# One channel tile of the depthwise convolution moves from VectorE to ScalarE and GpSimd, and the rotated queries get a new layout

## What is computed

```
h = rmsnorm(x, attn_norm_g)
q, k, v, conv_in, gate_logits = split(h @ w_in)        # 16 query heads of 64, 2 key/value heads
q, k = rope(q), rope(k)
y_attn = sliding_window_sink_attention(q, k, v) @ w_attn_o   # chunks of 64, window of 2 chunks
ca, cb = split(conv_in)
u = ca * sigmoid(cb)
u = causal_dwconv(u, conv_dw_w, conv_dw_b)             # 31 taps, one weight per channel and tap
y_conv = silu(layernorm(u)) @ w_conv_o
merged = sigmoid(g_attn) * y_attn + sigmoid(g_conv) * y_conv
x = x + merged @ w_out
h = rmsnorm(x, ffn_norm_g)
up = causal_dwconv(h @ w_ffn_up, ffn_dw_w)             # 3 taps
x = x + (silu(gate half) * value half) @ w_ffn_down
```

## Time and profile before

| what | value |
|---|---|
| median of three runs | 874.62 us (872.26 to 875.6) |
| the profiled execution, its own time | 872.64 us |
| its span, first to last instruction | 870.9 us |
| granted TensorE clock, mean | 0.994 of full speed |
| busy PE, DVE, ACT, POOL | 844.4, 627.4, 489.5, 396.4 us |
| instructions | 16394 |
| DMA | 142.26 MB, 163 GB/s |

### The profile page before, as it was taken

The page is one execution under the profiler, slowest core; times in us unless marked ns, Lnnn a source line. Parts: engine busy times, 40 slices in busy tenths (PEclk is TensorE's granted clock), DMA queues, the critical chain, the costliest instruction groups (busy, mean ns, idle before and its releaser), DMA issues.

```text
span 870.9 us, 16394 instructions
## 1 busy us (share of the span) xinstructions
PE 844.4 (97%) x6780; PEld 825.4 (95%) x6780; DVE 627.4 (72%) x1204; ACT 489.5 (56%) x754; POOL 396.4 (46%) x99
## 2 busy tenths in 40 slices
PE   8899999899999999999989999999999999999996
PEld 8899999799999999999979999989999999999996
DVE  6999999564568875666567899992636887666564
ACT  6536777473465464555563476774545555555452
POOL 4786656477403224222458785556571224222320
PEclk9999999999999999999999999999999999999999
DMA  7655433344454655554435544433454455554521
GB/s 262 207 192 170 170 129 119 140 145 146 146 195 145 198 189 194 193 172 170 148 126 211 180 160 146 146 131 113 145 190 135 160 194 194 194 183 161 191 96 49
DMA packets 22394, 142.26 MB, mean 163 GB/s; under 512 B 2736, under 2 KB 3248, under 8 KB 5808
## 3 DMA queue, kind: packets, MB, share of 16 engines
q1 hardware_dynamic: 21888, 140.96, 47.2%
q10 hardware_dynamic: 432, 0.26, 0.1%
HBM read 140.15 MB, written 1.05 MB: 162 GB/s over the span
## 4 chain that ended last, share of the span: by engine, by line
PE 66%; DVE 25%; ACT 6%; issue 2%; DMA 1%; POOL 1%; SPq 0%; DVEq 0%; ACTq 0%
PE pu L826 17%; PE pu L827 16%; PE pu L828 16%; DVE pc L594 11%; ACT whi L252 3%; DVE wlo L725 2%; PE ps L826 2%; PE ps L828 2%; PE ps L827 2%; PE ps L847 2%; PE po L847 2%; DVE qk L768 2%; PE pc L828 1%; PE pc L827 1%; PE pc L826 1%
## 5 line engine op out<-in xcount | busy, mean ns | idle before, releaser
L223 POOL TENSOR_TENSOR wlo<-raw,whi 128x2048 fp32r<-128x2048 f32 x83 | 382.6, 4612 | 435.9 <-ACT whi L252 435.9
L252 ACT ACTIVATE whi<-raw 128x2048 fp32r<-128x2048 f32 x129 | 245.5, 1903 | 19.0 <-PE pu L828 17.8
L826 PE MATMUL pu<-uh,whi 128*128 128x256 f32 x864 | 247.0, 286 | 3.5 <-DVE wlo L725 2.0
L827 PE MATMUL pu<-ul,whi 128*128 128x256 f32 x864 | 244.4, 283 | 0.0
L828 PE MATMUL pu<-uh,wlo 128*128 128x256 f32 x864 | 244.4, 283 | 0.0
L826 PE MATMUL pu<-hh,whi 128*128 128x256 f32 x768 | 221.6, 289 | 9.5 <-POOL wlo L223 5.9
L827 PE MATMUL pu<-hl,whi 128*128 128x256 f32 x768 | 218.7, 285 | 0.0
L828 PE MATMUL pu<-hh,wlo 128*128 128x256 f32 x768 | 218.5, 285 | 0.0
L594 DVE SCALAR_TENSOR_TENSOR pc<-upad,par_all,pc 128x256 f32<-128x256 f32 x464 | 186.5, 482 | 0.3
L826 PEld LDWEIGHTS pu<-uh,whi 128*128 128x128 f32 x864 | 165.7, 192 | 5.3 <-issue 4.9
L827 PEld LDWEIGHTS pu<-ul,whi 128*128 128x128 f32 x864 | 165.8, 192 | 0.2
(11 more groups left out here) (159 smaller groups left out, 1179.7 us busy)
## 6 DMA issues: line engine op xcount, KB each, us to landing
raw<-in_weights SPq DMA_DIRECT2D x129, 1024.0 KB, 4.9
raw<-in_weights SPq DMA_DIRECT2D x12, 256.0 KB, 7.0
x<-in_x_t SPq DMA_DIRECT2D x4, 256.0 KB, 5.2
out_y<-qk SPq DMA_DIRECT2D x4, 256.0 KB, 2.4
par_all<-in_params SPq DMA_DIRECT2D x1, 236.0 KB, 7.0
par_all<-in_params ACTq DMA_DIRECT2D x1, 236.0 KB, 2.4
probs<-in_positions SPq DMA_DIRECT2D x1, 128.0 KB, 6.8
const<-in_const SPq DMA_DIRECT2D x1, 64.0 KB, 7.2
```

Of the source, the lines that this page charges most:

```text
L223: nc.gpsimd.tensor_tensor(wlo[s][:, :], raw[s][:, :], whi[s][:, :].bitcast(f32), ALU.subtract).then_inc(lo_ready[s], 1)
L252: A(whi[s][:, :], raw[s][:, :], ACT.Copy).then_inc(hi_ready[s], 1)
L826: MM(out, whi[s][:, w], hi, start=start, stop=False, skip_group_check=accumulate)
L827: MM(out, whi[s][:, w], lo, start=False, stop=False, skip_group_check=accumulate)
```

## The change

Tile 2 of the eight leaves VectorE. ScalarE makes its 31 tap products, two to an instruction pair (`tap_product`), called from `next_high` at fourteen units of each layer, behind the copy of the weights; the first call makes two pairs and the last makes a pair and the single last tap. GpSimd adds each pair of 128 x 512 to a pair of sums (`add_products`), behind its subtraction for the same unit, then folds the two sums and adds the last product (`end_products`). ScalarE waits for the third addition back before it reuses one of three product buffers. VectorE has the pairs (0, 1), (3, 4), (5, 6) and then tile 7 alone as two half sums, 16 steps, the last of them an addition of the halves: 109 steps. In the softmax stage it does three steps where it did four. `mean_pair(1)` on TensorE waits for GpSimd's result as well.

The products and sums live in `qk[:, 2048:4096]`. To free that, `qr` becomes 128 partitions of 2048 columns: each rotated head stays on its own rows, so the addition of the rotation is one instruction of 128 rows for a query unit, and the keys are written twice, to both halves of the rows, by four instructions where there were two. Each scores matmul of 64 x 128 becomes two of 64 x 64, for the rows and the output partitions of the even and of the odd head.

```diff
-CONV_STEPS = TAPS * NT // 2
+CONV_PAIRS, POOL_TILE, LAST_TILE = ((0, 1), (3, 4), (5, 6)), 2, 7
+FIRST_TAPS = (TAPS + 1) // 2
+CONV_STEPS = TAPS * len(CONV_PAIRS) + FIRST_TAPS
+CONV_DONE = (2 * TAPS, 4 * TAPS, 6 * TAPS, 2 * CONV_STEPS)
+PRODUCT_BUFFERS = 3
+PRODUCT_UNITS = (7, 8, 9, 10, 11, 12, 14, 16, 17, 18, 19, 20, 21, 22)
+PRODUCTS = (TAPS + 1) // 2
+ADDITIONS = PRODUCTS - 1
...
-        qr = qk[0:HEAD_DIM, :].rearrange("p (i c o t) -> p i c o t", i=N_PAIRS, c=N_CHUNKS, o=2)
+        qr = qk[:, 0:2048].rearrange("p (i t) -> p i t", i=N_PAIRS)
+        two_sums = qk[:, 2048:2560].rearrange("p (a t) -> p a t", a=2)
+        products = [qk[:, 2560 + 512 * b:3072 + 512 * b].rearrange("p (a t) -> p a t", a=2) for b in range(PRODUCT_BUFFERS)]
-        kr = sb("kr", [HEAD_DIM, N_KV, T])
+        kr = sb("kr", [P, N_KV, T])
...
+            def add_products(l, n):
+                pool.wait_ge(tap_products, l * PRODUCTS + n + 2)
+                if n:
+                    pool.wait_ge(products_added, l * ADDITIONS + n)
+                nc.gpsimd.tensor_tensor(two_sums, two_sums, products[n % PRODUCT_BUFFERS], ALU.add).then_inc(products_added, 1)
+            def end_products(l):
+                n = PRODUCTS - 2
+                pool.wait_ge(products_added, l * ADDITIONS + n)
+                nc.gpsimd.tensor_tensor(two_sums[:, 0, :], two_sums[:, 0, :], two_sums[:, 1, :], ALU.add).then_inc(products_added, 1)
+                pool.wait_ge(tap_products, l * PRODUCTS + n + 2)
+                pool.wait_ge(products_added, l * ADDITIONS + n + 1)
+                nc.gpsimd.tensor_tensor(cv[:, POOL_TILE, :], two_sums[:, 0, :], products[n % PRODUCT_BUFFERS][:, 0, :], ALU.add).then_inc(pool_conv, 1)
...
                         split_low(s, l * USES + r)
+                        if r * RING + s in PRODUCT_UNITS:
+                            add_products(l, PRODUCT_UNITS.index(r * RING + s))
+                        if r * RING + s == PRODUCT_UNITS[-1]:
+                            end_products(l)
...
+                if u + RING in PRODUCT_UNITS:
+                    n = PRODUCT_UNITS.index(u + RING)
+                    if n == 0:
+                        tap_product(l, 0)
+                    tap_product(l, n + 1)
+                    if n == PRODUCTS - 3:
+                        tap_product(l, n + 2)
+            def tap_product(l, n):
...
+                if n == 0:
+                    act.wait_ge(par_ready, l * 5 + 1)
+                    act.wait_ge(u_ready, l * NT + POOL_TILE + 1)
+                elif n > PRODUCT_BUFFERS:
+                    act.wait_ge(products_added, l * ADDITIONS + n - PRODUCT_BUFFERS)
+                out = two_sums if n == 0 else products[(n - 1) % PRODUCT_BUFFERS]
+                for k in range(2 * n, min(2 * n + 2, TAPS)):
...
+                        last = A(out[:, k % 2, :], src, ACT.Copy, scale=w)
+                last.then_inc(tap_products, 1)
...
+                            if k == TAPS:
+                                dve.wait_ge(conv_step, l * 2 * CONV_STEPS + 2 * n + j)
+                                V.tensor_tensor(cv[:, t, :], pc[:, 0, :], cv[:, t, :], ALU.add).then_inc(conv_step, 1)
+                                continue
...
-                    for odd in range(2):
-                        rows = slice(64 * odd, 64 * odd + 64)
-                        split = [v[rows].rearrange("p n (c t) -> p n c t", c=N_CHUNKS) for v in (a, b)]
-                        V.tensor_tensor(outs[odd], split[0], split[1], ALU.add).then_inc(rope_done, 1)
+                    for rows, out in outs:
+                        last = V.tensor_tensor(out, a[rows], b[rows], ALU.add)
+                    last.then_inc(rope_done, 2)
...
-                    taps = (4, 4)
+                    taps = (3, 3)
...
-                        last = MM(bank[:, j, 0:keys.stop - keys.start], qr[:, GROUP_PAIRS * g + j, c, :, :],
-                                  kr[:, g, keys], start=True, stop=True)
+                        for odd in range(2):
+                            rows = slice(64 * odd, 64 * odd + 64)
+                            last = MM(bank[rows, j, 0:keys.stop - keys.start],
+                                      qr[rows, GROUP_PAIRS * g + j, CHUNK * c:CHUNK * c + CHUNK], kr[rows, g, keys], start=True, stop=True)
...
-                    sum_pair(ps[0][:, 0, :], cv, p, conv_step, (l * (NT // 2) + p + 1) * 2 * TAPS)
+                    if p == POOL_TILE // 2:
+                        pe.wait_ge(pool_conv, l + 1)
+                    sum_pair(ps[0][:, 0, :], cv, p, conv_step, l * 2 * CONV_STEPS + CONV_DONE[p])
```

More of the change, by code:

```diff
@@ L44 @@
 TAPS = CONV_WIDTH
-CONV_STEPS = TAPS * NT // 2
+CONV_PAIRS, POOL_TILE, LAST_TILE = ((0, 1), (3, 4), (5, 6)), 2, 7
[6 more added lines that the diff above has]
+ADDITIONS = PRODUCTS - 1
+assert len(PRODUCT_UNITS) == PRODUCTS - 2
 ROUNDING = 1.5 * 2.0 ** 23
@@ L141, in hybrid_encoder @@
         glu_tanh, u_ready, conv_step = sem("glu_tanh"), sem("u_ready"), sem("conv_step")
+        tap_products, products_added, pool_conv = sem("tap_products"), sem("products_added"), sem("pool_conv")
         kv_raw, rot_done, rope_ab, rope_done = sem("kv_raw"), sem("rot_done"), sem("rope_ab"), sem("rope_done")
@@ L256, in next_high @@
                     split_high(l, (u + RING) % RING, (u + RING) // RING)
+                if u + RING in PRODUCT_UNITS:
[6 more added lines that the diff above has]
+            def tap_product(l, n):
+                at = l * NPAR + PA_CW + POOL_TILE * CONV_WIDTH
+                bias = par_all[:, l * NPAR + PA_CB + POOL_TILE:l * NPAR + PA_CB + POOL_TILE + 1]
+                if n == 0:
[5 more added lines that the diff above has]
+                for k in range(2 * n, min(2 * n + 2, TAPS)):
+                    src, w = upad[:, POOL_TILE, k:k + T], par_all[:, at + k:at + k + 1]
+                    if k == 0:
+                        last = A(out[:, 0, :], src, ACT.Identity, scale=w, bias=bias)
+                    else:
+                        last = A(out[:, k % 2, :], src, ACT.Copy, scale=w)
+                last.then_inc(tap_products, 1)
             def high_piece(s, p):
@@ L581, in conv @@
                     for n in range(first, last):
-                        pair, k = n // TAPS, n % TAPS
+                        pair = n // TAPS
                         for j in range(2):
-                            t = 2 * pair + j
+                            if pair < len(CONV_PAIRS):
+                                t, k, begins, ends = CONV_PAIRS[pair][j], n % TAPS, n % TAPS == 0, n % TAPS == TAPS - 1
+                            else:
+                                t, k = LAST_TILE, n % TAPS + FIRST_TAPS * j
+                                begins, ends = n % TAPS == 0, k == TAPS - 1
+                            if k == TAPS:
+                                dve.wait_ge(conv_step, l * 2 * CONV_STEPS + 2 * n + j)
+                                V.tensor_tensor(cv[:, t, :], pc[:, 0, :], cv[:, t, :], ALU.add).then_inc(conv_step, 1)
+                                continue
                             w = par[:, PA_CW + t * CONV_WIDTH + k:PA_CW + t * CONV_WIDTH + k + 1]
@@ L588, in conv @@
                                 dve.wait_ge(conv_step, l * 2 * CONV_STEPS + 2 * n + j - 1)
-                            if k == 0:
+                            if begins:
                                 dve.wait_ge(u_ready, l * NT + t + 1)
+                            if begins and k == 0:
                                 V.tensor_scalar(sums, upad[:, t, 0:T], w, par[:, PA_CB + t:PA_CB + t + 1], ALU.mult, ALU.add).then_inc(conv_step, 1)
+                            elif begins:
+                                V.tensor_scalar(sums, upad[:, t, k:k + T], w, None, ALU.mult).then_inc(conv_step, 1)
                             else:
-                                out = sums if k < TAPS - 1 else cv[:, t, :]
+                                out = cv[:, t, :] if ends else sums
                                 V.scalar_tensor_tensor(out, upad[:, t, k:k + T], w, sums, ALU.mult, ALU.add).then_inc(conv_step, 1)
@@ L619, in rotate @@
                     dve.wait_ge(rope_ab, l * 10 + 2 * n + 2)
-                    for odd in range(2):
-                        rows = slice(64 * odd, 64 * odd + 64)
-                        split = [v[rows].rearrange("p n (c t) -> p n c t", c=N_CHUNKS) for v in (a, b)]
-                        V.tensor_tensor(outs[odd], split[0], split[1], ALU.add).then_inc(rope_done, 1)
+                    for rows, out in outs:
+                        last = V.tensor_tensor(out, a[rows], b[rows], ALU.add)
+                    last.then_inc(rope_done, 2)
                 dve.wait_ge(act_table, 2)
                 dve.wait_ge(kv_raw, l + 1)
-                rotate(0, pu[U_KV % RING][:, 0:1, :], 1, HEAD_DIM ** -0.5, [kr[:, g:g + 1, :].rearrange("p n (c t) -> p n c t", c=N_CHUNKS) for g in range(N_KV)])
```

(3 more changed lines are left out.)

## The result

The changed kernel takes 866.54 us (median of 4 runs, 865.75 to 868.95) against 874.05 for the kernel before in the same measurement: ratio 0.9917, 95% interval 0.9899 to 0.9935. With more rounds, in another measurement, it was 867.89 against 874.41: 0.993, 0.9913 to 0.9947. All runs of the two kernels together: 867.48 (10 runs) and 874.43 (52 runs), a difference of 6.9 us.

A forecast was written before the change was run, and what follows sets the result against it. TensorE was taken as the bound, busy 844.4 of 870.9 us. From the profiled 872.64 us, -2.0 for stalls and 0 for scores gave 870.6, moved to 872.6 against the median 874.62; range 868.5 to 880.

The forecast's parts named there:

- most of the 13 us less a layer on VectorE: Convolution and rotation: some 13 us a layer leave VectorE, nearly all beside a full TensorE, worth nothing by itself.
- ScalarE's and GpSimd's work is hidden: Products and additions of tile 2: taken as 0; the mean's second pair covered by 2 to 3 us.
- the tiles work side by side: Scores: two column tiles run together, so eight records in each take what eight took, 0 us.
- the stalls of group 7: TensorE's waits before group 7's transposes and the values behind: 1.2 us back in layer 0, 0.8 in layer 1, together 2.0.
- The 4.9 us that I gave to layer 0: Layer 0, transposes of group 6 to group 7: 5.33 us becomes 4.50 plus 0.4 for ScalarE's later copy.
- I take 0 for the 16 groups.: Scores of all groups: twice the matmuls in two tiles side by side cost and save nothing, 0 us.
- the lower end, -2 us: Scores from below: with 64 keys the time halves, 4 x -0.5 = -2 us.
- a rival with 0.10: Faster side: all softmax stalls go and short scores get shorter, 4.4 + 2 = 6.4 us, 868.2; chance 0.10.
- 4.4 us is the most that a free VectorE can give back: TensorE's softmax waits: 3.1 us for the output's low part and 1.3 for the probabilities, each twice, cap the gain.
- the sum: Whole kernel: profiled 872.64 us with -2.0 + 0 gives 870.6; 2.0 under the median, so 872.6 against 874.62.
- TensorE's waits for VectorE's softmax results are two.: Softmax stage: one wait at the end of each layer's stage; between 100 and 150 us TensorE doesn't stop.
- The two rules of the Trainium skill: Scores: loads overlap only other row groups (878 us, chance 0.08); different row tiles cannot share a PSUM bank, making turns.

The follow-up runs named there:

- The layout alone: Kernel before with only the new layout of rotated queries and keys and scores in 64 x 64 tiles, whole convolution on VectorE: 871.03 us, ratio 0.9959.
- the products alone: Changed kernel with the old layout, four scores matmuls of 64 x 128 a group, products in a tile of their own: 869.65 us, ratio 0.9952.

## Why the prediction was wrong

Right: TensorE is the bound, but for the third stall below, and most of the 13 us less a layer on VectorE are worth nothing by themselves; ScalarE's and GpSimd's work is hidden; the tiles work side by side. The gain came from the places that the prediction named, the stalls of group 7 and the scores, but two of its steps priced them too low.

- *The stalls.* Forecast 2.0 us. The waits went from 4.4 to 2.1, so 2.3, and the values came 1.43 us behind the transposes in both layers, as forecast (1.44). The 4.9 us that I gave to layer 0 were 4.51: I added ScalarE's products to the end of a copy that started late, at 152.29, because ScalarE had waited 1.19 us for VectorE's denominators. That wait fell to 0.17. The copy, and the three products in 1.30 us behind it, now read:

```profile
151.35 1.91 ACT L283 ACTIVATE whi<-raw 128x2048 fp32r<-128x2048 f32 x1
153.16 1.30 ACT L311 ACTIVATE qk<-upad,par_all 128x256 f32<-128x256 f32 x3
155.16 0.60 ACT L419 ACTIVATE probsT<-pt 128x512 f32<-128x512 f32 x1 [0.70 <-PE pt L970]
```

- *GpSimd.* Tile 2 was forecast ready at 161.8 us; it was at 160.87, 3.8 us before the mean's first matmuls, at 164.68:

```profile
157.90 1.29 POOL L241 TENSOR_TENSOR qk<-qk 128x512 f32<-128x512 f32 x1
159.26 0.73 POOL L247 TENSOR_TENSOR qk<-qk 128x256 f32<-128x256 f32 x1
160.13 0.74 POOL L250 TENSOR_TENSOR cv<-qk 128x256 f32<-128x256 f32 x1
```

- *The scores, a step that failed: a term at nothing.* "I take 0 for the 16 groups." The 4 groups with 64 keys save 1.03 - 0.61 = 0.42 us each, the 12 with 128 keys 1.08 - 1.02 = 0.06: 2.4 us. I had the lower end, -2 us, and the row that leads to it: half the keys saved nearly nothing, so the loads set the pace there, and the loads were to be halved and shared by two tiles. To leave it out of the likeliest case, and give it to a rival with 0.10, was the error of weighing. The layout alone measured 3.4 us, with the 0.8 of the transposes' wait in it.
- *The stalls' price, the other step that failed: "4.4 us is the most that a free VectorE can give back".* A stall was priced at its own length. It also lowers the clock behind it, in about half of the runs of before, in both layers, which costs 1.5 us in layer 1 and at least 2.6 in layer 0. The profiled execution that the sum was made against was one without it. I noted that it lay 2.0 us under the median and moved the sum up by as much, as if that were chance. It is the difference between one kind of run and the median of both kinds, and most of it goes with the change: no run of the changed kernel has a mean clock under 0.992, and neither of its traces has the lower clock at the end of the softmax stage. The two traces differ by 2.3 + 2.4 = 4.7 us, nearly all of their 4.9. The median of all runs of before is 2.1 us above the median of those with 0.994, and 4.7 + 2.1 = 6.8 is the 6.9 us measured.
- *"TensorE's waits for VectorE's softmax results are two."* That is so in a short run. A long one has the third, 1.0 us in the middle of the stage, and the change takes it away too. How the 2.1 us are shared between this wait and the clock is not shown.
- *The two rules of the Trainium skill.* The records of a group start in pairs, one for each head's rows, 0.007 us apart. With 128 keys a pair follows the last by 0.109 us, where the records of 64 x 128 followed each other by 0.112; with 64 keys by 0.058, where it was 0.112. By the Trainium skill, "TensorE: Matmul & The Clock Gate", Part 3, a load would not overlap matmuls of its own rows. The trace disagrees: in the program's order, the load at 131.817 is for the rows whose matmul is shown from 131.815 to 132.084, and between the pairs there is no room for a load. By the Trainium skill, "TensorEngine Tiling (Array Packing)", Gotcha 1, different row tiles cannot use one PSUM bank at once. The trace disagrees here too, since each pair writes one bank; the two outputs lie on different partitions of it.

Shown: that the stall brings the lower clock in part of the runs (put back, it came back; taken out or filled, it went), and that the change keeps the stall short enough in the traces taken. Not shown: that the lower clock never follows it in the changed kernel. Four of its ten runs have a mean of 0.992, its two traces 0.995 and 0.997, and a mean doesn't say where the clock was low. Why a run is of one kind or the other is open too.

## What to carry to other kernels

Look at the spread of the runs, and at the mean granted clock of each, before trusting one trace. Where that clock has two values, some traces have something that the one at hand has not, and a change may take away just that. A stall of TensorE costs its length and, at times, a stretch at half the clock; shorten it, or fill it with matmuls that nobody reads, which was worth 1.8 to 2.8 us here at the layers' starts. And when a row says that a cost isn't set by the size one thinks of, the change to the size that does set it has to be priced.

## What was not expected of the hardware

- Idle of 1.6 us before the last but one values, with 1.1 or 0.26 us some 2 us earlier, was followed by a granted clock of 0.5 (1.2 GHz) in 2 of 5 traces of the kernel before, in both layers of the same run; idle of 0.78 us in place of 1.6 was not, in three traces (two of the changed kernel, one of the products alone). Both long traces had a clock of 1.00 at 34 to 38 us, the three short ones a lower one there.
- Two 64 x 64 tiles on different rows and different output partitions of one PSUM bank ran side by side: sixteen records with 64 keys in 0.61 us, 0.04 a record, where eight 64 x 128 ones took 1.03.
- GpSimd's 128 x 512 additions took 1.30 us and VectorE's convolution instructions kept their 0.39 us from start to start beside them (six in 2.42 us, 0.48 for one, after; eight in 3.20 in the earlier trace rows).
